# Adding four blocks pairwise in place of one tensor_reduce, and one mean matmul per token piece in place of two, in the RMSNorms of a two-layer decoder step

## The reference

```
def rmsnorm(x, g):
    xf = x.astype(jnp.float32)
    y = xf * lax.rsqrt(jnp.mean(xf * xf, axis=-1, keepdims=True) + EPS)
    return (y * g.astype(jnp.float32)).astype(x.dtype)

def trunk(x, ...):
    for layer in range(DEPTH):
        h = rmsnorm(x, norm_mix[layer])
        if layer % 2 == 0:
            ...                      # gated convolution and sliding-window attention
        else:
            yc, pbuf = pool_mix(h, pool_st[i], pos0, w_pool[i], pool_scale[i])
            x = x + yc
        x = x + sqrelu_mlp(rmsnorm(x, norm_mlp[layer]), w_up[layer], w_down[layer])
```

## Time and profile before

| what | value |
|---|---|
| median of three runs | 2044.31 us (2041.98 to 2044.43) |
| span of the profiled execution | 2043.0 us |
| PE / PEld busy | 2004.9 us (98%) / 1959.0 us (96%) |
| DVE / ACT / POOL busy | 967.2 us (47%) / 539.9 us (26%) / 45.5 us (2%) |
| chain that ended last | PE 91%, DVE 6%, ACT 2%, issue 1% |
| reduction of squares, L1371 | 24 times, 64.6 us, 2692 ns each |

### The profile page before, as it was taken

One profiled execution on the slowest core, in us unless ns is written; L12 is line 12 of the kernel. 1 busy time (PEld: TensorE's weight loads), 2 busy tenths in 40 slices (PEclk: granted clock), 3 DMA queues, 4 the chain that ended last, 5 costly groups with the idle time before them and its releaser, 6 DMA issues.

```text
span 2043.0 us, 30495 instructions
## 1 busy us (share of the span) xinstructions
PE 2004.9 (98%) x12458; PEld 1959.0 (96%) x12458; DVE 967.2 (47%) x1604; ACT 539.9 (26%) x965; POOL 45.5 (2%) x88
## 2 busy tenths in 40 slices
PE   6999999999999999999999999999999999999999
PEld 5888888999999999999999999999999999999998
DVE  5777776484333333333333487633333333333433
ACT  5333333143122121213121333313121221212131
POOL 1210000100000000000000000000000000000000
PEclk8899999999999999999999998999999999999999
DMA  5411101312111120211211110111211111211112
GB/s 204 146 47 32 32 32 58 99 42 61 42 42 41 41 62 21 62 41 41 62 41 42 42 42 5 31 53 41 62 41 41 41 41 41 62 31 51 52 32 85
DMA packets 132336, 106.42 MB, mean 52 GB/s; under 512 B 4771, under 2 KB 126919, under 8 KB 132240
## 3 DMA queue, kind: packets, MB, share of 16 engines
q1 hardware_dynamic: 126800, 90.52, 14.7%
q0 software_dynamic: 5216, 14.78, 2.3%
q10 hardware_dynamic: 248, 0.09, 0.0%
HBM read 94.64 MB, written 10.49 MB: 51 GB/s over the span
## 4 chain that ended last, share of the span: by engine, by line
PE 91%; DVE 6%; ACT 2%; issue 1%; DMA 0%; SPq 0%; DVEq 0%; ACTq 0%
PE out L525 29%; PE out L527 28%; PE out L526 28%; PE out L950 2%; PE turned L744 1%; DVE norm_sum L1371 1%; DVE head_sq L1427 1%; PE turned L727 1%; DVE act_lo L1394 1%; PE scores L693 1%; PE turned L581 0%; DVE w_lo L1361 0%; DMA raw<-in_w_in_even 0%; DVE rs L1386 0%; ACT act_hi L1052 0%
## 5 line engine op out<-in xcount | busy, mean ns | idle before, releaser
L525 PE MATMUL out<-act_hi,w_hi 128*128 128x352 f32 (+1 forms) x2160 | 714.9, 331 | 6.5 <-DVE qT L1433 2.8
L527 PE MATMUL out<-act_hi,w_lo 128*128 128x352 f32 (+1 forms) x2160 | 703.1, 326 | 0.0
L526 PE MATMUL out<-act_lo,w_hi 128*128 128x352 f32 (+1 forms) x2160 | 700.9, 325 | 0.0
L525 PE MATMUL out<-hid_hi,w_hi 128*128 128x352 f32 (+1 forms) x1536 | 501.3, 326 | 0.0
L527 PE MATMUL out<-hid_hi,w_lo 128*128 128x352 f32 (+1 forms) x1536 | 499.6, 325 | 0.0
L526 PE MATMUL out<-hid_lo,w_hi 128*128 128x352 f32 (+1 forms) x1536 | 497.7, 324 | 0.0
L525 PEld LDWEIGHTS out<-act_hi,w_hi 128*128 128x128 f32 x2160 | 408.3, 189 | 19.3 <-issue 12.3
L526 PEld LDWEIGHTS out<-act_lo,w_hi 128*128 128x128 f32 x2160 | 409.0, 189 | 1.4 <-issue 0.2
L527 PEld LDWEIGHTS out<-act_hi,w_lo 128*128 128x128 f32 x2160 | 408.2, 189 | 0.0
L1636 DVE TENSOR_TENSOR residual<-out,residual 128x352 f32<-128x352 f32 (+1 forms) x408 | 213.1, 526 | 399.2 <-PE out L527 398.8
L1011 ACT ACTIVATE w_hi<-raw 128x1024 fp32r<-128x1024 f32 x156 | 161.2, 1052 | 633.6 <-PE out L527 632.9
(11 more groups left out here) (172 smaller groups left out, 928.4 us busy)
## 6 DMA issues: line engine op xcount, KB each, us to landing
raw<-in_w_up SPq DMA_DIRECT2D x64, 512.0 KB, 4.2
raw<-in_w_down SPq DMA_DIRECT2D x64, 512.0 KB, 3.5
raw<-in_w_in_even SPq DMA_DIRECT2D x18, 512.0 KB, 3.9
raw<-in_w_out_even SPq DMA_DIRECT2D x8, 512.0 KB, 3.5
out_y_prompt<-y_rows SPq DMA_DIRECT2D x8, 512.0 KB, 2.7
x_rows<-in_x_prompt SPq DMA_DIRECT2D x7, 512.0 KB, 7.5
x_spill<-residual POOLq DMA_DIRECT2D x2, 1408.0 KB, 6.1
x_again<-x_spill POOLq DMA_DIRECT2D x16, 176.0 KB, 2.6
```

The lines of the kernel that those rows point to most:

```text
L525: nc.tensor.matmul(out, lhs[0], rhs[0], start=first, stop=False)
L526: nc.tensor.matmul(out, lhs[0], rhs[1], start=False, stop=False)
L527: return nc.tensor.matmul(out, lhs[1], rhs[0], start=False, stop=last)
```

## The change

In `norm_reduce`, each half's four blocks are added pairwise: blocks 0 and 1 plus blocks 2 and 3 in one instruction of twice the width, in place in `norm_buf`, and then the two results into `norm_sum[:, half_]`. For the second half a third add puts the two halves' sums together in `norm_sum[:, 0]`. `then` is a helper that makes DVE wait on a semaphore of its own until the instruction before has written. The wait for `norm_mean` (PE has read the sums of the piece before) stays on the first half only. In `norm_stats`, PE makes one matmul on `norm_sum[:, 0]` where it made two, and the same for each column of n = 2. The order of steps, the DMAs and all other waits stay.

```
-                        for half_ in range(2):
-                            ins_ = nc.tensor.matmul(turned2[0:t1 - t0, col:col + 1], norm_sum[:, half_, t0 - c0:t1 - c0],
-                                                    const[:, C_MEAN:C_MEAN + 1], start=half_ == 0, stop=half_ == 1)
+                        ins_ = nc.tensor.matmul(turned2[0:t1 - t0, col:col + 1], norm_sum[:, 0, t0 - c0:t1 - c0],
+                                                const[:, C_MEAN:C_MEAN + 1], start=True, stop=True)
                     ins_.then_inc(norm_mean, 1)
                     return
-                for half_ in range(2):
-                    ins_ = nc.tensor.matmul(turned2[:, 0:c1 - c0], const[:, C_MEAN:C_MEAN + P],
-                                            norm_tensors(n)[1][:, half_, 0:c1 - c0], start=half_ == 0, stop=half_ == 1)
-                ins_.then_inc(norm_mean, 1)
+                nc.tensor.matmul(turned2[:, 0:c1 - c0], const[:, C_MEAN:C_MEAN + P],
+                                 norm_tensors(n)[1][:, 0, 0:c1 - c0], start=True, stop=True).then_inc(norm_mean, 1)
...
                 buf, total = norm_tensors(n)
+                w = c1 - c0
                 dve.wait_ge(norm_sq, i + 1)
-                if i >= 2:
+                if i >= 2 and half_ == 0:
                     dve.wait_ge(norm_mean, i // 2)
-                nc.vector.tensor_reduce(total[:, half_, 0:c1 - c0], buf[:, :, 0:c1 - c0].rearrange("p c n -> p n c"),
-                                        AX_X, ALU.add).then_inc(norm_summed, 1)
+                then(nc.vector.tensor_tensor(buf[:, 0:2, 0:w], buf[:, 0:2, 0:w], buf[:, 2:4, 0:w], ALU.add))
+                if half_ == 0:
+                    nc.vector.tensor_tensor(total[:, 0, 0:w], buf[:, 0, 0:w], buf[:, 1, 0:w], ALU.add)\
+                        .then_inc(norm_summed, 1)
+                    return
+                then(nc.vector.tensor_tensor(total[:, 1, 0:w], buf[:, 0, 0:w], buf[:, 1, 0:w], ALU.add))
+                nc.vector.tensor_tensor(total[:, 0, 0:w], total[:, 0, 0:w], total[:, 1, 0:w], ALU.add)\
+                    .then_inc(norm_summed, 1)
```

## The result

The changed kernel takes 2025.49 us (median of 4 runs, 2024.64 to 2029.75), the kernel before on the same chip 2044.37 (4 runs, 2041.98 to 2046.7): a ratio of 0.9909, with an interval of 0.9897 to 0.9921.

What follows compares the result with a forecast made beforehand. PE was taken to bound the kernel, busy 2004.9 of 2043.0 us. Savings of 5.47 + 2.91 + 1.88 + 3.72 = 14.0 us gave a span of 2029.0, and with 1.3 for the median 2030.3 us; range 2026 to 2037.5.

Steps and rivals of the forecast that it cites:

- Price of the adds: DVE's adds, read off a line through two other shapes: 0.89 us for 704 columns, 0.525 for 352.
- Rival A: DVE's adds run at the reduction's pace, 2.23 us per first half; 7.2 us saved, 2037 us; chance 0.11.
- Norm 0: First 75 us, PE waiting on DVE and ACT: earlier sums and one saved matmul give 5.47 us over three pieces.
- Norm 1 and norm 2: Norm 1: PE's 1.14 us wait goes and three matmuls are saved, 2.91 us; norm 2: only matmuls halved, 1.88 us.
- Norm 3: Pooling mixer: PE's waits of 0.96 and 0.33 us go and one matmul per piece is saved, 3.72 us.
- the sum of 14.0: Total saving over norms 0 to 3: 5.47 + 2.91 + 1.88 + 3.72 us.
- The clock: Pooling mixer, 1215 to 1285 us: shifted timing may change where PE's lower clock falls, 2 us either way.
- Rival B: Fewer gaps keep PE's clock up behind waits in the mixer and before m = 7; 2026 to 2028 us; chance 0.08.
- Rival B's other place: Norm 0: output m = 7, behind PE's wait at 73.38, runs at the full clock level.
- The price of the reduction: DVE's reduction takes 1.77 ns per number because of its reading order; L1512, reading neighbours, costs the same as an add.
- Rivals C and D: C: A plus overstated matmul savings, 2040.7 us, chance 0.05. D: pooling mixer wholly at lower clock, 2076 us, chance 0.04.

Runs made afterwards that it cites:

- hybrid: The changed kernel, but two mean matmuls and no third add for norm 0's second and third pieces; 2022.84 us (0.9899) and 2023.44 us (0.9897) against the kernel before.

## Why the prediction came out low

- **Price of the adds**: right, 0.886 and 0.525 us. Rival A would have had 2.23 us for a first half; it took 1.45.
- **Norm 0**: right. 5.47 us predicted; 5.11, 5.41 and 5.36 in three profiles against the first of before. The two `hybrid` profiles show that a third add on the path costs its own 0.57 there, as the term has it.
- **Norm 1 and norm 2**: right, 2.9 and 1.8 us. The wait of 1.14 us is gone in all three profiles; how narrow the margin was is not measured.
- **Norm 3**: the step that failed. "Which covers 0.96 + 0.33 = 1.29" counted the waits at their own length. The mechanism is right, both waits go, but the term is mis-sized: taking these waits away alone gave 4.3 us and putting waits back cost 3.9, since PE also runs at 1.2 GHz for longer when it waits (granted clock of the stretch 0.86 to 0.91 with the waits in the kernel before, 0.93 without). That alone lifts the sum of 14.0 by some 2.8, to a time of 2027.5 us. The three profiles of the change show 5.3 against 3.72, because its first one met the lower level (0.88) without a wait.
- **The clock**: the section had it as 2 us "either way". For the mixer it should have leaned one way: nothing was added there, and in both pairs of kernels the waits went with a lower clock on average. A single execution still goes either way (70.2 us beside 67.2 for the change). Rival B named the mechanism and the place, and its 2026 to 2028 us is the nearest forecast, though the kernel landed 0.5 below it; it had been given 0.08. No row of before had a price for it: the earlier trace rows shows that the lower level is there for a third of the stretch, not that the waits bring it. It took a kernel with the waits taken away. The Trainium skill (TensorE: Matmul & The Clock Gate, section "Why this matters for your kernels") warns of idle gaps between bursts of matmuls, but of longer ones than any wait in this mixer. The measurement goes beyond it: the waits of 0.8 to 1.3 us in the table above cost some 3 us beyond themselves on average (4.3 - 1.1 and 3.9 - 0.9).
- **Rival B's other place**, the wait before m = 7: that wait got longer, and no run tests what stands behind it. The 0.7 us gained there are 1.8, 0.1 and 0.1 in the change's three profiles. Some 1.6 us come in four of the twelve profiles with adds in norm 0 and in none of the eight with reductions, so it is something that the adds allow and one execution in three shows.
- **What is left**: the mis-sized term gives 2027.5, inside the range; the median is 2.0 below that. In the profiles, 2.7 us came in stretches for which nothing was predicted (0.7 behind m = 7, 1.0 in the attention, 1.1 in the mixer's column, -0.1), and norm 3 fell 1.2 short of the 6.5 that its term has with the waits at 4.1. Much of this is chance of single executions, as shown above. But on three chips the medians are 18.9, 18.4 and 19.4 us apart, each time more than 14.0 + 2.8 = 16.8, though each interval reaches down to that. What the last 2 us hang on stays open.
- **The price of the reduction**: that it is dear "because of its order of reading" is argued, not shown. L1512, which the prediction sets beside it, reads neighbours, but it also makes 4 results where L1371 makes 352, and no run tells the two causes apart. The sum does not need it.
- **Rivals C and D**: neither came. No wait for weights appeared, and the second MLP only starts earlier (-0.1 us).

## What to carry to other kernels

Where PE waits for about a microsecond in a stretch whose granted clock is already below full, price the wait at what the stretch gains when it goes, here about four times its length on average, and try it by lengthening or shortening the one instruction that PE waits for. A reduction of a few numbers that lie far apart, for each of many results, can be worth replacing by adds of contiguous blocks, though they are more instructions: here 3.47 us for 5.31. Two parts of a change can need each other: the single matmul saves time only because the adds have made room for the third add.

## What the runs showed of the hardware that was not expected

- Executions of the same code differ in where PE's clock falls: three profiles of the kernel before have spans of 2043.0, 2039.0 and 2043.2 us, and the change ran from 2023.06 to 2029.75. A difference under 4 us between two profiles says nothing without a look at which stretch it lies in.
- In one profile a wait of 0.81 us was followed by 32 matmuls of 5.28 us that take 3.64 without it; so the wait cost more behind it than in it. In two others the same wait was followed by 4.25 and 3.71.
- A wide add in place, with the same buffer as source and target, costs no more than one between two buffers: 886 ns for 704 columns, on the line of the others.
